# Thirty-two experts in another order of tile sizes: one run of 96-slot experts, then the 64-slot ones

## The reference

```python
logits = (t @ router_w) + router_b
top_v, top_e = lax.top_k(logits, TOP_K)          # 4 of 32
gate = jax.nn.softmax(top_v, axis=-1)
...
gu = t_pad[tok] @ w_up[e] + b_up[e]
a = jnp.minimum(gu[:, :D_FF], SWIGLU_LIMIT)
u = jnp.clip(gu[:, D_FF:], -SWIGLU_LIMIT, SWIGLU_LIMIT)
y = ((u + 1.0) * a * jax.nn.sigmoid(SWIGLU_ALPHA * a)) @ w_down[e] + b_down[e]
out = out.at[slot_tok].add(y * g)
```

## Time and profile before

| | |
|---|---|
| median of 3 runs | 1723.56 us (1721.05 to 1726.95) |
| the profiled execution: its time | 1721.29 us |
| its span, first to last instruction | 1719.6 us |
| TensorE matmul busy | 1644.5 us (96%) |
| VectorE / ScalarE / POOL busy | 30% / 27% / 11% |
| DMA | 499.61 MB; 296 GB/s over the span |
| weights of experts by SP (L656) | 384 halves of 1 MB, 25.1 us from issue to landing (median) |

### The profile page before, as it was taken

One profiled execution on the slowest core, in us unless ns is written; L12 is line 12 of the kernel. 1 busy time (PEld: TensorE's weight loads), 2 busy tenths in 40 slices (PEclk: granted clock), 3 DMA queues, 4 the chain that ended last, 5 costly groups with the idle time before them and its releaser, 6 DMA issues.

```text
span 1719.6 us, 44351 instructions
## 1 busy us (share of the span) xinstructions
PE 1644.5 (96%) x19448; PEld 1400.9 (81%) x19448; DVE 521.9 (30%) x1278; ACT 465.9 (27%) x930; POOL 193.9 (11%) x263
## 2 busy tenths in 40 slices
PE   7999999999998999998798999998999998899998
PEld 4899988788777778975445899995799996699996
DVE  6866785655446855100000000000000000000000
ACT  5245654534323432121111121111111111112111
POOL 0023000003322133100000000000000000000000
PEclk9999999999999999999999999999999999999999
DMA  5064232124437329899999999999999999999996
GB/s 216 33 214 122 87 125 99 50 62 135 119 99 279 119 99 360 322 371 407 410 408 402 404 403 402 408 396 392 409 398 405 406 403 391 403 407 399 400 406 250
DMA packets 99341, 499.61 MB, mean 291 GB/s; under 512 B 15198, under 2 KB 32694, under 8 KB 48496
## 3 DMA queue, kind: packets, MB, share of 16 engines
q1 hardware_dynamic: 84288, 458.39, 67.5%
q0 software_dynamic: 14768, 38.71, 8.2%
q10 hardware_dynamic: 144, 0.55, 0.1%
HBM read 485.61 MB, written 22.73 MB: 296 GB/s over the span
## 4 chain that ended last, share of the span: by engine, by line
PE 79%; DMA 12%; DVE 4%; issue 2%; SPq 1%; ACT 1%; POOL 0%; DVEq 0%; POOLq 0%; ACTq 0%
PE bank L1351 22%; PE bank L1349 13%; DMA ring<-in_w_exp 10%; PE bank L1346 7%; PE bank L833 7%; PE bank L733 5%; PE bank L888 5%; PE bank L760 3%; PE bank L1343 2%; PE bank L1152 2%; SPq L656 1%; PE bank L1408 1%; PE bank L700 1%; PE bank L901 1%; PE bank L922 1%
## 5 line engine op out<-in xcount | busy, mean ns | idle before, releaser
L1351 PE MATMUL bank<-ring,slab 128*32 128x128 f32 x5664 | 630.5, 273 | 0.0
L1349 PE MATMUL bank<-ring,slab 128*32 128x384 f32 x5664 | 622.8, 487 | 2.9 <-DMA ring<-in_w_exp 2.3
L1351 PEld LDWEIGHTS bank<-ring,slab 128*32 128x32 f32 x5664 | 613.5, 110 | 0.0
L2636 DVE TENSOR_SCALAR slab<-bank 128x384 f32<-128x384 f32 (+2 forms) x64 | 33.0, 516 | 920.8 <-PE bank L1351 594.5
L1346 PE MATMUL bank<-ring,slab 128*64 128x256 f32 x2080 | 242.3, 385 | 28.7 <-DMA ring<-in_w_exp 28.2
L1346 PEld LDWEIGHTS bank<-ring,slab 128*64 128x64 f32 x2080 | 146.0, 138 | 114.5 <-DMA ring<-in_w_exp 40.0
L1349 PEld LDWEIGHTS bank<-ring,slab 128*32 128x32 f32 x5664 | 212.1, 109 | 10.1 <-issue 4.4
L1865 ACT ACTIVATE slab<-bank 128x384 f32<-128x384 f32 (+2 forms) x64 | 29.3, 457 | 446.4 <-PE bank L1351 292.9
L833 PE MATMUL bank<-ring_rounded 128*128 128x260 f32 x768 | 147.7, 291 | 0.0
L833 PEld LDWEIGHTS bank<-ring_rounded 128*128 128x128 f32 x768 | 117.8, 188 | 14.0 <-issue 11.9
L2776 POOL DMA_INDIRECT slab<-token_rows,small x31 | 31.0, 999 | 572.3 <-PE bank L1338 531.8
(11 more groups left out here) (549 smaller groups left out, 2202.1 us busy)
## 6 DMA issues: line engine op xcount, KB each, us to landing
ring<-in_w_exp SPq DMA_DIRECT2D x378, 1024.0 KB, 25.1
ring<-in_w_blk SPq DMA_DIRECT2D x40, 512.0 KB, 3.6
slab<-in_w_tok SPq DMA_DIRECT2D x4, 1304.0 KB, 15.1
ring<-in_w SPq DMA_DIRECT2D x8, 512.0 KB, 3.5
ring<-in_w_out SPq DMA_DIRECT2D x2, 2048.0 KB, 16.5
xn<-in_w_exp SPq DMA_DIRECT2D x4, 1024.0 KB, 11.1
xn<-in_xT SPq DMA_DIRECT2D x4, 520.0 KB, 7.6
ring<-in_k_cmp SPq DMA_DIRECT2D x32, 64.0 KB, 3.6
```

The source lines that it names most:

```text
L1349: mm(bank[32 * g:32 * g + 32, c, 0:384], rows(32 * g, 32), w[:, 0:384], start=first, stop=last)
L1351: r = mm(bank[96:128, c, P * g:P * (g + 1)], rows(32 * g, 32), w[:, 384:512], start=first and g == 0, stop=last and g == 2)
```

## The change

`CAP` is ordered anew: the two first places as before, then all eighteen other 96-slot places, four of 64 slots, the one of 128, seven of 64. The numbers of places are the same (20 of 96, 11 of 64, 1 of 128), so the same experts get the same sizes; only their order in time differs. TensorE's loops follow: sixteen 96-slot blocks in one loop, three and six 64-slot blocks in two others, the rest written out, and no loop within a loop. All other engines follow from `CAP`.

```diff
-CAP = (MID, MID) + 4 * (FEW,) + (P,) + 3 * (2 * (FEW,) + 6 * (MID,)) + (FEW,)
+CAP = 20 * (MID,) + 4 * (FEW,) + (P,) + 7 * (FEW,)
...
-            block_of(1, MID, FEW)
-            block_of(2, FEW, FEW)
-            with pe.Fori(0, 2) as i:
-                block_of(i + 3, FEW, FEW)
-            block_of(5, FEW, P)
-            block_of(6, P, FEW)
-            with pe.Fori(0, 3) as t:
-                block_of(8 * t + 7, FEW, FEW)
-                block_of(8 * t + 8, FEW, MID)
-                with pe.Fori(0, 5) as i:
-                    block_of(8 * t + (i + 9), MID, MID)
-                block_of(8 * t + 14, MID, FEW)
+            block_of(1, MID, MID)
+            block_of(2, MID, MID)
+            with pe.Fori(0, 16) as i:
+                block_of(i + 3, MID, MID)
+            block_of(19, MID, FEW)
+            with pe.Fori(0, 3) as i:
+                block_of(i + 20, FEW, FEW)
+            block_of(23, FEW, P)
+            block_of(24, P, FEW)
+            with pe.Fori(0, 6) as i:
+                block_of(i + 25, FEW, FEW)
             block_of(NE - 1, FEW, None)
```

## The result

Before: 1723.56 us (1721.05 to 1726.95). After: **1742.97 us** (1735.48 to 1744.9), a ratio of 1.0097 with a 95% interval of 1.007 to 1.0124. Timed once more, beside the kernel before on one chip (r1_change_again), the change gave 1741.02 against 1724.98 us, 1.0093 (1.0067 to 1.012). The profiled execution of the change has a span of 1733.7 us and is the fastest of its three: the part ahead of the experts happened to be 5 us shorter in it (block 1's mark is at 734.09 instead of 739.09). From that mark to the end of the span it is 999.6 us, against 980.5 before: **+19.1 us in the experts' stage**. r1_change_again has 1000.1 us there, although its whole span is 5.3 us longer, so this stretch is the steadier measure.

The account below looks back on a forecast made before the run. The weights' DMA queue, 32.88 us per expert, was taken as the limit. Block 20's start at 1362.4, last landing at 1730.5 and 8.9 us more gave +19.8; profiled 1721.29 + 19.8 = 1741.1, median 2.3 higher: 1743, range 1732 to 1751.

Parts of the forecast that it names:

- The total: Whole span: ends at 1739.4 us, 19.8 us later; median of runs predicted at 1743 us.
- The head: Part ahead of the experts: block 1's mark, POOL's gather in mid-block, stays at 739.09 us.
- The long run: Blocks 1 to 19, all 96 slots: marks 34.05 us apart at TensorE's pace, block 19's at 1352.0.
- The queue idle: Weights' queue in the 96-slot run: idle 1.17 us per block, issue to landing falling to 5 to 8 us.
- The tail: Blocks 20 to 31: queue-limited at 32.88 us per expert, 359.0 us in sum, last half landing at 1730.5.
- The block of 128 slots: Place 24: at most 39.70 us on TensorE, 7 us slower than the queue at most, leaving no queue gap.
- The end: Behind the last landing: matmuls, scaling and the last add take 8.9 us, unchanged.
- The pauses at nothing: TensorE's outer-loop branches, places 15 and 23: "issue" pauses of 5.12 and 5.02 us go, gaining nothing.
- Rival A: Experts' stage: TensorE's own time sets the end, so removing both pauses gives 1713.4 us; chance 0.04.
- rival B: Weights' queue: not idle in the long run, total the same in any order, about 1724 us; chance 0.08.
- rival C: Small-block run: TensorE's clock falls to half, eight blocks adding some 100 us; chance 0.03.
- The rule on interleaving regimes: Order of block sizes: advises interleaving regimes whose most contended engine differs, so speaks against this change, which separates them.

Follow-up runs that it names:

- c2: Changed kernel reordered: two 96-slot blocks, four of 64, the 128, eighteen of 96, seven of 64; 1730.46 us against 1724.98 before.
- c7: Changed kernel reordered into two runs of nine 96-slot blocks, each behind smaller blocks, with single loops; 1725.45 us against 1724.32 before.
- c4: Kernel before, small blocks spread: seven times two of 96 slots and one of 64, looped over three blocks; 1742.88 us against 1725.78.
- c5b: Order of c4, but blocks written out except one loop over four 96-slot blocks; 1736.3 us against 1724.8 before.
- c6b: Order of the kernel before, every TensorE block written out, differing from c1 only in having no loops; 1733.26 us against 1724.8 before.
- e1: Changed kernel with its loop of sixteen 96-slot blocks nested, so the outer loop branches back three times; 1776.51 us against 1725.78 before.
- d1: Changed kernel loading only a quarter of the last half of weights of experts 4 to 19; 1742.1 us against 1725.24 before.
- d2: Changed kernel loading only a quarter of the last half of weights of experts 21 to 31; 1720.41 us against 1725.24 before.
- c1: Order of the kernel before, TensorE's nested loop replaced by written-out blocks and single loops; 1724.11 us against 1724.98 before.
- c3: Changed kernel reordered: two 96-slot blocks, eleven of 64, the 128, then eighteen of 96 to the end; 1755.49 us against 1724.98 before.

## Why the prediction was right, point by point

- **The total.** The sum was 19.8 us in the experts' stage; the profiles have 19.1 and 19.6. That the median came out at 1742.97 against a forecast of 1743 is luck: the three runs spread over 9.4 us, and the second timing gave 1741.02.
- **The head.** "Block 1's mark stays at 739.09" was 734.09 in the profiled execution and is taken out in what follows; in the other profiles here it lies from 738.5 (c2 and c7) to 749.3 (c4), latest in the four kernels with most TensorE code fetched (c4, c5b, c6b, e1: 744.4 to 749.3). The forecast took it as fixed, and whether the code causes that was not tried.
- **The long run.** 34.05 us per block, block 19's mark 612.9 us behind block 1's: measured 612.75.
- **The queue idle.** Time to landing of 5 to 8 us: measured 6.9 to 8.7. d1 shows that the queue had time to spare; it also moved 386 GB/s here, where it moved 404 in the same kind of blocks before (990 to 1126).
- **The tail.** From block 19's mark to the last landing I had 1730.5 - 1352.0 = 378.5 us; measured 1724.60 - 1346.84 = 377.8. The pace of 32.88 us holds as a mean; the last small blocks go at 32.55. d2 shows the queue as the limit.
- **The block of 128 slots** was misread. The distance of two marks is not the length of a block when the neighbours differ in size: 39.70 us was called its upper bound, and it takes 44.0 (rows at c2). It is 11 us slower than the queue and not "7 us at most", and the average block on TensorE is 30.5 us, not 30.4. The sum doesn't use it, and the backlog ahead of it was large enough: what is issued during it (1467 to 1511) still takes 24.9 us to land. In c2 and c7 the run behind this block was expected to start with a full backlog, and the first had 15.8 us.
- **The end.** 8.9 us behind the last landing; measured 1733.7 - 1724.6 = 9.1.
- **The pauses at nothing.** Shown by c1. The rule on taken branches of the Trainium skill, page "Runtime: NRT & Kernel Launch", section on instruction fetch mechanics, holds as to the stall, at all places where code of several blocks was branched over. That removing it gives nothing back here is the queue's doing; in e1, where TensorE is the limit, it costs in full.
- **Rival A** falls with c1, **rival B** with landing times of 7 to 9 us in the long run and with d1, **rival C** with the clock of 0.99 to 1.00 in the tail.
- **The rule on interleaving regimes** of the Trainium skill, page "Perfetto Trace Analysis", section on optimization strategy, is borne out in direction by the change, c2 and c3. c4 and c5b show its bound: mixing more finely than before gave nothing, and cost code.

Two of the signs that the prediction named were wrong. I expected the DMA share to fall to 0.97 of its value; it reads 1.01, for the reason above. And I expected waits for weights of 75 to 85 us in the row of TensorE's matmuls; it has 53.8. The loss is there: from block 20's start to the last landing, 1724.6 - (1346.84 + 10.4) = 367.4 us pass. At their own pace the blocks need 11 x 22.88 + 44.0 = 295.7 us, of which 2.0 come behind the landing, so 73.7 us are lost. Part of it is booked under the weight loads (78.4 us), whose idle time overlaps the matmuls'. The row of one kind alone undercounts.

## What to carry to other kernels

Where two resources take turns as the limit and a buffer of fixed depth lies between them, order matters through the backlog (loads issued and not yet landed): measure it at the start and end of each run of equal work. Avoid a long run in which the consumer is the slower side and which begins with a small backlog, and avoid an end at which the consumer has much work left when the last load has landed. An idle stretch or a pause is worth nothing by itself; ask what its engine would do next, and whether that waits anyway. Then try it alone, as c1 did, since the same kind of pause was free in one order and cost 11 us in another.

## What was not expected of the hardware

- TensorE's program is fetched by DMA, in packets of 16 KB, beside the weights. Code that needs sixty more of them (0.98 MB) made the stage 10.4 us longer (c6b against c1, one profile each); at the mean rate of about 400 GB/s they should take 2.5. Why it costs four times that is open. That they fall on few of the 16 engines would fit, since the kernel counts a half as landed only with the last of 16 signals (`then_inc(signal, 16)`), but the trace doesn't name the engine of a packet and it wasn't tried. Nor is it shown why 18 fewer fetches in c7 gave nothing.
- The queue of weights lost pace before it was empty: 403 GB/s with 21 to 29 us of backlog, 393 with 16 falling to 11 (c7).
- A branch back over several blocks paused TensorE once each time, for 5.1 and 5.0 us, in the kernel before, but twice, for 5.2 and 3.2 us, in e1, where the granted clock stood at 0.50 (1.2 GHz) for 10.2 us. That e1 branches to a 96-slot block with its longer code is not the reason: c4 does so too and pauses once each time, for 4.9 to 5.2 us. What makes the second pause is open.
- A DMA share of 1.01 was shown both by a queue with 29 us from issue to landing and by one with 7.
